# A rebuilt routing chain between the output product and the experts of a mixture-of-experts encoder

## What is computed

```python
def hier_moe(h, ...):                      # h = rms_norm(x, ln_ffn), 512 tokens x 1024
    g_logits = xf @ w_gr + b_gr            # 4 groups
    grp = top_k(g_logits, 1)
    e_logits = xf @ w_er + b_er            # 32 experts, 8 in a group
    top_v, top_i = top_k(e_logits of that group, 2)
    gate = softmax(g_logits)[grp] * softmax(top_v)
    # every expert e on its own tokens: (silu(x @ w_gate[e]) * (x @ w_up[e])) @ w_down[e]
    # out[token] += gate * expert output
```

## Time and profile before

| | |
|---|---|
| median of 3 runs | 1386.55 us (1379.8 to 1386.73) |
| profiled execution, its own time | 1388.14 us |
| its span in the profile | 1386.3 us |
| busy share PE, PEld, DVE, ACT, POOL | 90%, 59%, 40%, 30%, 16% |
| granted TensorE clock, mean | 0.967 |
| chain that ended last: PE, DMA, DVE, ACT | 75%, 10%, 6%, 3% |
| DMA | 278 MB, mean 201 GB/s |

### The profile page before, as it was taken

How to read it: one execution, slowest core, us unless ns; L and a number is a source line. 1 busy time by engine, 2 the same in 40 slices (tenths; PEclk the granted TensorE clock), 3 DMA queues, 4 the chain that set the end, 5 groups by cost and what they waited for, 6 DMA issues and landing times.

```text
span 1386.3 us, 15934 instructions
## 1 busy us (share of the span) xinstructions
PE 1248.8 (90%) x5822; PEld 818.4 (59%) x5822; DVE 551.3 (40%) x848; ACT 414.5 (30%) x809; POOL 215.7 (16%) x214
## 2 busy tenths in 40 slices
PE   4998879999975999999899898899999579999997
PEld 4975557777763444444388655577778434444443
DVE  3345552344242233333464455434342513333335
ACT  3425662222121212222251356422231112212223
POOL 1333540000002111110204325200000031111000
PEclk9999999999995999999999999999999779999999
DMA  9503003332056999999903120043310869999991
GB/s 279 171 16 91 1 1 107 91 91 76 31 206 266 396 415 416 416 414 417 344 2 125 28 64 1 2 150 92 91 62 16 328 257 415 415 416 416 417 412 78
DMA packets 119448, 278.44 MB, mean 201 GB/s; under 512 B 12976, under 2 KB 74928, under 8 KB 102992
## 3 DMA queue, kind: packets, MB, share of 16 engines
q1 hardware_dynamic: 111680, 259.00, 49.4%
q0 software_dynamic: 6400, 13.74, 3.0%
q10 hardware_dynamic: 1296, 4.72, 0.9%
HBM read 279.51 MB, written 8.40 MB: 208 GB/s over the span
## 4 chain that ended last, share of the span: by engine, by line
PE 75%; DMA 10%; DVE 6%; ACT 3%; issue 3%; DVEq 1%; ACTq 1%; SPq 1%; POOL 0%; POOLq 0%
PE bank L1156 70%; DMA arena<-w_up 5%; DMA ring<-w_up 3%; PE bank L1404 2%; PE bank L1277 2%; ACT arena L743 1%; PE bank L1173 1%; DMA x<-x_prompt 1%; DVE arena L833 1%; DVE small L973 1%; DMA arena<-token_rows,idx 1%; ACT arena L747 1%; SPq L472 0%; PE bank L1443 0%; DVE arena L968 0%
## 5 line engine op out<-in xcount | busy, mean ns | idle before, releaser
L1156 PE MATMUL bank<-arena 128*64 128x512 f32 (+5 forms) x1442 | 329.6, 517 | 34.6 <-DVEq L1115 15.0
L1156 PEld LDWEIGHTS bank<-arena 128*64 128x64 f32 (+2 forms) x1442 | 153.2, 156 | 186.3 <-issue 133.5
L1156 PE MATMUL bank<-ring,arena 128*64 128x512 f32 (+1 forms) x800 | 190.6, 607 | 7.0 <-issue 2.5
L1156 PE MATMUL bank<-y_parts,chosen 128*128 128x512 f32 x512 | 135.2, 408 | 5.5 <-DVE y_parts L1139 5.3
L1156 PEld LDWEIGHTS bank<-ring,arena 128*64 128x64 f32 (+1 forms) x800 | 64.5, 142 | 121.5 <-issue 121.5
L608 POOL MEMSET arena<- 128x1024 f32 x32 | 30.7, 959 | 657.7 <-DVEq L1125 448.0
L1094 DVE TENSOR_TENSOR x<-x,bank 128x512 f32<-128x512 f32 x128 | 87.9, 687 | 61.6 <-PE bank L1156 61.6
L1156 PEld LDWEIGHTS bank<-y_parts,chosen 128*128 128x128 f32 x512 | 92.2, 191 | 28.1 <-issue 8.7
L1156 PE MATMUL bank<-hT_gate_low,w_chunk_high 128*128 128x512 f32 x256 | 103.8, 406 | 3.5 <-issue 3.1
L1156 PE MATMUL bank<-hT_gate_high,w_chunk_low 128*128 128x512 f32 x256 | 102.0, 399 | 0.0
L1156 PE MATMUL bank<-hT_gate_high,w_chunk_high 128*128 128x512 f32 x256 | 101.8, 398 | 0.0
(11 more groups left out here) (209 smaller groups left out, 1846.0 us busy)
## 6 DMA issues: line engine op xcount, KB each, us to landing
ring<-w_gate SPq DMA_DIRECT2D x32, 1024.0 KB, 14.5
ring<-w_up SPq DMA_DIRECT2D x32, 1024.0 KB, 18.8
ring<-w_down SPq DMA_DIRECT2D x32, 1024.0 KB, 18.9
arena<-w_gate SPq DMA_DIRECT2D x32, 1024.0 KB, 15.9
arena<-w_up SPq DMA_DIRECT2D x32, 1024.0 KB, 20.1
arena<-w_down SPq DMA_DIRECT2D x32, 1024.0 KB, 19.7
ring<-w_in SPq DMA_DIRECT2D x36, 512.0 KB, 6.6
ring<-w_in SPq DMA_DIRECT2D x4, 1024.0 KB, 12.7
```

Of the source, the lines that this page charges most:

```text
L1156: return pe.matmul(out, lhsT, rhs, start=first, stop=last)
```

## The change

The router no longer works on normalised rows. PE transposes x itself (`token_transposes`, half a chunk at a time, the left half before the chunk's right half is complete); x^T is the stationary operand and the 36 columns of `w_router`, which DVE has multiplied by the gain beforehand (a new small input, `ffn_gain`), stream. DVE applies 1/rms and the bias in one step (`token_logits`). The transposes and router chunks are put between the parts of the output products. The normalised rows are still made and stored for the gather.

The rank matmuls and the token table run on fp32r operands in a single pass, on a copy of the triangle and ones that POOL makes. A choice's slot is found with a key: the rank plus 0 or 1000 for either half of the pair; one comparison with 0 to 63 marks the slot. Token values are token - 512, so that an empty slot gives 512 after the addition, which is out of bounds. The weights get a table matmul of their own (two-pass), behind the token table, with a semaphore of their own (`w_slot_ready`). The pass count comes before the ranks are used. POOL clears the four row buffers during the output products and again at the end of a pass; only pairs 4 to 15 are cleared inside. `gate_up` waits for the first half of the transposed rows and, four steps later, for the second. `mark_slots` for a possible further pass runs at pair 8.

```diff
+                sp.dma_start(gain_k, ffn_gain[l]).then_inc(params_in, 16)
@@ POOL
+                pool.wait_ge(dense_used, l * USED + 14)
+                pool.nop(nofuse=True)
+                pool.tensor_copy(tri_ones, cst[:, P:3 * P]).then_inc(tri_ones_ready, 1)
+                for b in range(4):
+                    pool.memset(xrows[:, b, :], 0.0)
+                pool.drain()
                 pool.wait_ge(passes_ready, l + 1)
...
-                        pool.memset(xrows[:, r % 4, :], 0.0)
-                        pool.drain()
+                            pool.memset(xrows[:, r % 4, :], 0.0)
+                            pool.drain()
                         pool.indirect_dma_start(out=xrows[:, r % 4, :], out_offset=None, in_=token_rows,
...
+                    for b in range(4):
+                        pool.wait_ge(xs_ps, seen * (2 * PAIRS) + (2 * (PAIRS - 4 + b) + 2))
+                        pool.nop(nofuse=True)
+                        pool.memset(xrows[:, b, :], 0.0)
+                    pool.drain()
@@ ACT
-                for c in range(C + 1):
-                    if c < C:
-                        act.wait_ge(x_mixed, l * 8 + 5 + c)
-                        norm_root(c)
+                for c in range(C):
+                    act.wait_ge(hT_ps, l * 16 + (2 * c + 9))
+                    act.activation(hT[:, 0:4, c * P:(c + 1) * P], bank[1 + c % 2][:, :].rearrange("p (k t) -> p k t", k=4), ACT.Copy).then_inc(hT_act, 1)
+                    act.wait_ge(x_mixed, l * 8 + 5 + c)
+                    norm_root(c)
                     if c >= 1:
-                        norm_copy(l * 2 + 1, c - 1)
+                        act.wait_ge(h_ready, l * 8 + 4 + c)
                         act.dma_start(token_rows[(c - 1) * P:c * P, :], htok_flat[:, c - 1, :]).then_inc(rows_out, 16)
-                act.wait_ge(logitsT_ps, l + 1)
-                act.activation(logitsT[0:NG + NE, :], bank[4][0:NG + NE, :], ACT.Copy).then_inc(logitsT_done, 1)
+                act.wait_ge(h_ready, l * 8 + 4 + C)
+                act.dma_start(token_rows[(C - 1) * P:C * P, :], htok_flat[:, C - 1, :]).then_inc(rows_out, 16)
@@ DVE
+            def token_evac(l, c):
+                dve.wait_ge(hT_ps, l * 16 + (2 * c + 10))
+                dve.tensor_copy(hT[:, 4:8, c * P:(c + 1) * P], bank[3][:, :].rearrange("p (k t) -> p k t", k=4)).then_inc(hT_dve, 1)
+
+            def token_logits(l, c):
+                dve.wait_ge(router_ps, l * C + c + 1)
+                dve.scalar_tensor_tensor(out=route_[:, c * (NG + NE):(c + 1) * (NG + NE)], in0=bank[4 * (c == C - 1)][:, 0:NG + NE],
+                                         scalar=rstd[:, c:c + 1], in1=b_router[:, :], op0=ALU.mult, op1=ALU.add).then_inc(logits_done, 1)
...
+                dve.tensor_tensor(w_router[:, :, :], w_router[:, :, :], gain_k.unsqueeze(2).broadcast_to([P, KD, NG + NE]), ALU.mult).then_inc(router_ready, 1)
                 dve.wait_ge(hT_whole, l + 1)
...
                 for o in range(8):
+                    c, n = o % 4, o // 4
+                    if n == 1 and c >= 1:
+                        token_evac(l, c - 1)
+                        norm_chunk(l * 2 + 1, c - 1)
                     dve.wait_ge(out_ps, l * 8 + o + 1)
...
+                    if n == 1 and c >= 1:
+                        token_logits(l, c - 1)
+                token_evac(l, C - 1)
+                norm_chunk(l * 2 + 1, C - 1)
+                token_logits(l, C - 1)
...
+                halves = picked.rearrange("p k c (r e) -> p k c r e", e=2)
+                dve.tensor_reduce(odd, halves[:, :, :, :, 1], AX.X, ALU.add)
+                step(dve.tensor_tensor(one_pair, halves[:, :, :, :, 0], halves[:, :, :, :, 1], ALU.add))
+                dve.tensor_scalar(key_off[:, :, :, 0], odd, 1000.0, None, ALU.mult)
+                dve.tensor_scalar(key_off[:, :, :, 1], odd, -1000.0, 1000.0, ALU.mult, ALU.add)
+                dve.tensor_tensor(token_vals, one_pair, token.unsqueeze(1).unsqueeze(3).broadcast_to([P, 2, C, PAIRS]), ALU.mult)
+                dve.wait_ge(ranks_ps, l + 1)
...
+                step(dve.tensor_tensor(key, key_off, rank.unsqueeze(3).broadcast_to([P, 2, C, 2]), ALU.add))
+                def mark_slots():
+                    dve.tensor_tensor(at_slot_r.rearrange("p k c (b s) -> p (k c) b s", b=2),
+                                      iota[:, 0:BLK].unsqueeze(1).unsqueeze(1).broadcast_to([P, 2 * C, 2, BLK]),
+                                      key.rearrange("p k c b -> p (k c) b").unsqueeze(3).broadcast_to([P, 2 * C, 2, BLK]), ALU.is_equal)
+                    dve.drain().then_inc(table_ready, 1)
...
+                    dve.tensor_scalar(idx[:, :], bank[7][:, 0:PAIRS], float(T), None, ALU.add).then_inc(table_done, 1)
@@ PE
+                def token_transposes(c, half):
+                    pe.wait_ge(x_mixed, l * 8 + (5 + c if half else 4))
...
+                    for k in range(4):
+                        t = pe.transpose(b[:, k * P:(k + 1) * P], x[:, c, (4 * half + k) * P:(4 * half + k + 1) * P], ident)
+                    t.then_inc(hT_ps, 1)
...
+                    for k in range(4 * half, 4 * half + 4):
+                        m = mm(bank[4 * (c == C - 1)][:, 0:NG + NE], hT[:, k, c * P:(c + 1) * P], w_router[:, k, :], k == 0, k == KD - 1)
...
                 for c in range(C):
-                    out_product(2, c, True, False)
-                    out_product(3, c, False, True).then_inc(out_ps, 1)
-                    if c == C - 1:
-                        pe.drain().then_inc(dense_used, 1)
+                    out_product(2, c, range(4), True, False)
                     if c >= 1:
-                        norm_transposes(l * 2 + 1, c - 1)
-                    if c >= 2:
-                        route_chunk(c - 2)
+                        token_transposes(c - 1, 1)
+                    token_transposes(c, 0)
+                    out_product(3, c, range(2), False, False)
+                    if c >= 1:
+                        if c == 1:
+                            pe.wait_ge(router_ready, l + 1)
+                        route_chunk(c - 1, 0)
+                        route_chunk(c - 1, 1).then_inc(router_ps, 1)
+                    out_product(3, c, range(2, 4), False, True).then_inc(out_ps, 1)
+                pe.drain().then_inc(dense_used, 1)
+                route_chunk(C - 1, 0)
+                token_transposes(C - 1, 1)
+                route_chunk(C - 1, 1).then_inc(router_ps, 1)
...
-                mm(bank[7][:, 0:(C + 1) * NE], tri, both, True, False)
+                mm(bank[7][:, 0:(C + 1) * NE], tri_ones[:, 0:P], picks, True, False)
...
-                            m = mm(bank[7][:, 0:2 * PAIRS], at_slot[:, k, c, :], slot_values[:, k, c].rearrange("p v r -> p (v r)"),
-                                   k == 0 and c == 0, k == 1 and c == C - 1)
+                            m = mm(bank[7][:, 0:PAIRS], at_slot_r[:, k, c, :], token_vals[:, k, c, :], k == 0 and c == 0, k == 1 and c == C - 1)
                     m.then_inc(table_ps, 1)
+                    pe.wait_ge(weights_ready, l + 1)
+                    for k in range(2):
+                        for c in range(C):
+                            m = mm(bank[6][:, 0:PAIRS], at_slot_r[:, k, c, :].bitcast(F32), one_pair[:, k, c, :], k == 0 and c == 0, k == 1 and c == C - 1)
+                    m.then_inc(weights_ps, 1)
```

More of the change, by code:

```diff
@@ L179, in encoder_kernel @@
         xsT_, _ = take(2 * KD * P)
-        at_slot_, _ = take(2 * C * P)
+        at_slot_, at_slot_at = take(2 * C * P)
         chosen_at = Place.at
@@ L185, in encoder_kernel @@
         hidT_, _ = take(2 * FC * P)
-        route_, _ = take(1088)
-        logitsT, _ = take(T)
+        route_, route_at = take(1088)
+        tables_, tables_at = take(T)
         end_ffn = Place.at
@@ L1026, in _ @@
                 me, oh1, oh2 = (route(224 + 128 * i, NE, 1) for i in range(3))
-                both, none = route(608, NE, 1), route_[:, 608 + C * NE:608 + (C + 1) * NE]
+                both, none = picks[:, 0:C * NE].rearrange("p (c n) -> p c n", c=C), picks[:, C * NE:(C + 1) * NE]
                 prod = route_[:, 800:800 + 2 * C * NE].rearrange("p (k c n) -> p k c n", k=2, c=C)
                 picked = route_[:, 352:352 + 2 * C * NE].rearrange("p (k c n) -> p k c n", k=2, c=C)
-                dve.memset(none, 0.0)
+                dve.memset(none.bitcast(F32), 0.0)
                 def wide(v, n):
@@ L1061, in _ @@
                 dve.drain().then_inc(picks_ready, 1)
+                halves = picked.rearrange("p k c (r e) -> p k c r e", e=2)
[5 more added lines that the diff above has]
+                dve.wait_ge(ranks_ps, l + 1)
+                step(dve.tensor_reduce(most, bank[7][:, C * NE:(C + 1) * NE], AX.X, ALU.max))
+                step(dve.tensor_scalar(overs, over, most, None, ALU.is_lt))
+                step(dve.tensor_reduce(npf, overs, AX.X, ALU.add))
+                dve.tensor_copy(passes[:, :], npf)
```

(47 more changed lines are left out.)

116 lines of the change are left out of this document (34 added, 82 removed).

## The result

The changed kernel takes 1364.5 us (median of 4 runs, 1361.75 to 1372.49), the kernel before 1386.6 beside it (1379.8 to 1389.4). The ratio is 0.987, with a 95% interval of 0.984 to 0.990: 18 us faster, 13 to 23; the two medians differ by 22.1. The forecast was 12.2 us faster, 1374.5 us, with a range of 1366 to 1383. The profiled execution took 1361.75 us, 26.4 less than the profiled one before.

What follows compares the result with a forecast made beforehand. The expert loop was held by TensorE and the DMA engines within 3%; TensorE's smaller gain of 6.5 us a layer, less 0.4, gave 6.1, 12.2 in all, hence a 1374.5 us median (range 1366 to 1383).

Steps and rivals of the forecast that it cites:

- T moves 5.1 later: End of the last output product, when DVE's add starts: extra transposes and router chunks delay it 5.1 us (2.7 to 8.7).
- The dear router: Rival, router chunks ahead of T: weight loads at 0.188 us move T 8.7 us; gain 2.5 a layer, 1381.5; chance 0.18.
- T to the logits 4.4: From the last output product to the router logits: 4.4 us instead of 10.2, saving 5.8 us.
- Picks to table_ready 5.5 for 10.0: From the end of expert picking to the slot table's start: 5.5 us instead of 10.0, saving 4.5.
- Table 0.9 less, indices 1.4, clears 1.4: Slot table to gather issue: table matmuls save 0.9 us, DVE's index step 1.4, POOL's clear and drain 1.4.
- Gather 8.0: First row gather, now under full weight loads: 8.0 us instead of 4.9, losing 3.2 (bounds 0 and 4.3).
- The rows did not queue behind the weights: Rival at the gather: rows served only after queued weight loads, landing at 442.8, total 1396 us; chance 0.06.
- The sum on TensorE's side: Routing stage up to the first expert product: terms sum to 6.5 us a layer gained, before 0.4 for scaling router weights.
- The clock: TensorE's granted clock, 0.50 when the gathered rows arrive: an earlier return was mentioned but given no gain.
- The waits of the loop: TensorE's waits for weights in the expert loop, about 3.5 us a layer before: would grow slightly.
- the cap: Weight stream: starts 5.1 us later, loses 12.3 us idle; the DMA side would limit the gain to 7.2 us a layer.
- The race: Rival at layer 0's end: DVE's `chosen` gets ahead of POOL's subtraction, 5.3 us more won, 1369 us; chance 0.17.

Runs made afterwards that it cites:

- fenced profiles: Profiles of the kernel before and the changed kernel, each with the fence added; medians 1377.7 and 1361.7 us.
- f_clears: Clears and drains put back ahead of every gather, against the changed kernel with the fence (1361.7 us): 1364.98 us.
- the fence: One wait added to either kernel: POOL splits the next layer's first weights only after the last `chosen`; before 1377.7 us, changed 1361.7 us.
- f_warm2: Unused matmuls (8, 3 and 9) fill TensorE's routing pauses, against the changed kernel with the fence (1361.7 us): 1361.98 us.

## Why the prediction was right, and where it was off

The direction, the path and most terms were right. The size was not, and part of what the plain runs gained is a race that I had given 0.17.

- **T moves 5.1 later.** 4.55 in both layers (last adds minus the first add of the stage: 404.33 - 365.26 against 398.72 - 364.20). The steps from add to add give the parts: 5.60 us without any insert, 6.46 with eight transposes, 8.53 with eight transposes and the old router chunk, 8.24 with eight and the new one. So a new router chunk added 1.8, as taken, the old one 2.1 for my 1.9, and twelve transposes 1.3 for my 1.6. The dear router did not come.
- **T to the logits 4.4.** 4.1. The scaling on DVE is what the logits wait for, as said.
- **Picks to table_ready 5.5 for 10.0.** 5.1, from the end of the last picking step (415.16) to 420.27. Ranks 1.22 for 1.7.
- **Table 0.9 less, indices 1.4, clears 1.4.** Table to indices 2.48 for 3.66, so 1.2; indices to the gather's issue 1.10 for 3.61, so 2.5 for my 2.8.
- **Gather 8.0.** 8.6. The median of all 32 is 8.2; of the first four the last took 13.6, and TensorE waited for the first alone. The rows did not queue behind the weights.
- **First product 0.85.** 0.94 (432.45 to 434.35 for 437.79 to 440.63).
- **The sum on TensorE's side, 6.5 less 0.4 for the router weights.** To the first product 41.9 - 30.0 - 4.55 - 0.7 = 6.6, in layer 1 5.9. The scaling of the router weights took 0.74 us (0.90 in layer 1), and in layer 0 the copies behind it came 0.7 later: 0.7 for my 0.4.
- **The clock, priced at nothing.** It was back 5 us after the rows came, where it had taken 8, and the first product took 8.5 us for 9.9 (in layer 1 7.95 for 8.8). This term was mis-sized: 1.4 and 0.9 us, and 0.9 and 1.0 in the two fenced profiles.
- **The waits of the loop "grow slightly".** This step failed, and with it the cap that the DMA side was to set at 7.2 us a layer. The waits shrank, by 1.9 and 1.1 us (228.7 to 226.9, 229.5 to 228.4), in the fenced profiles by 1.1 and 0.8; and the fenced kernels gain 8.7 and 7.7 us a layer, more than 7.2. I had counted the three gathers as a charge on the backlog. In the trace of before the third and fourth went out at 443.88 and 448.04, during the first product and beside the refills; now they are issued ahead of it. `f_clears` puts them back and its loops are 0.7 and 1.5 us longer, which is in keeping with that but not clear of the 1 us by which loops differ. What made the waits shrink stays open.
- **The race, 0.17.** It was a rival and turned as described, by a slip of 1.15 us. I had priced it at the 5.3 us of TensorE's wait; with the slower product behind it, it is 6.6 in the traces and 7.0 by the fence. That it may also turn from run to run I had not seen, though the runs of before, 1379.8 beside 1386.55 and 1386.73, had hinted at it. Of the 14.2 us that the profiled execution gained over the sum, 6.6 are the race.

Together: 8.7 and 7.7 us a layer by the fenced profiles (last adds to last silu, less the 4.55 and 0.7), 16.4 against 16.0 of the medians. Of these TensorE's way to the first product is 12.6, which is the 12.2 of my sum; the clock is 1.8 and the loop's waits are 1.9. That the first part comes so close is in part luck: in layer 0 the stages up to the table's end won 1.5 us more than I took (0.8, 0.4 and 0.3), and what follows 1.1 less (0.3 at the issue, 0.5 in the gather, 0.3 for the scaling). The working of TensorE's side stands; on the DMA side the cap and the growing waits do not.

## What to carry to other kernels

Cost a chain ahead of a DMA-heavy loop on both sides, when the engine can start and when the stream can, and don't take the smaller of the two for a cap. Here 4.55 us of router work ahead of the last adds, with 0.7 for the weights' scaling, ate the 5.1 us that the new router had won behind them; holding back loads for the sake of one gather lost 7.7 us; and moving one product behind the point that starts the loads gave the lowest median. Look at the spread of single runs before taking any of it for noise: times 7 us apart were two outcomes of one race, and a wait of one line fixed the outcome.

## What the runs showed of the hardware

- A VectorE comparison with both inputs in SBUF took 6.9 to 7.5 us instead of 0.68 when a GpSimd subtraction over 3328 elements had begun less than a microsecond earlier (683.98 behind 683.70; 674.44 behind 673.56), and 1.32 when it began 0.8 us before the end of a GpSimd copy. The Trainium skill ("SBUF — State Buffer", "Who interferes with whom") states that a VectorE instruction with two SBUF inputs contends with a GpSimd instruction that reads SBUF, under an exclusive lock. The traces agree: the later one waits for the whole instruction, VectorE here, and GpSimd by 0.46 us (7.68 for 7.22) where it came second.
- Four indirect gathers were in flight at once: issued 1.3 to 1.4 us apart, without a drain between them, they landed after 8.6, 10.9, 12.2 and 13.6 us. With a clear and a drain between them each was issued only some 0.9 us after the one before had landed (432.91 + 4.8, next at 438.60; in `f_clears` 421.41 + 8.9, next at 431.16).
- With filling matmuls in its pauses (`f_warm2`) TensorE won only 1.7 us on the way to the first silu of layer 0 and lost 0.9 in layer 1. The rows began to be transposed 28.2 us after the adds where it had been 28.3. Even so the granted clock fell, to a mean of 0.61 from 420 to 424 us, behind the table's matmuls, which stream 16 columns each.
